# Where the sums of the first feed-forward's down projection read from, and the order of GpSimd's factor sums

## What is computed

```python
def swiglu(u, w_gate, w_up, w_down):
    return (jax.nn.silu(u @ w_gate) * (u @ w_up)) @ w_down
...
u = rmsnorm(h, ffn_norm[layer])
h = h + swiglu(u, *[p[layer] for p in ffn_p])
```

## Time and profile before

| | before |
|---|---|
| median of 3 runs | 3046.07 us (3045.73 to 3047.8) |
| profiled execution, its own time | 3044.75 us |
| its span, first to last instruction | 3042.9 us |
| PE busy | 2966.7 us (97%) |
| DVE, ACT, POOL busy | 1925.5, 1179.0, 1526.2 us |
| mean granted TensorE clock | 0.992 of full speed |

### The profile page before, as it was taken

How to read it: one execution, slowest core, us unless ns; L and a number is a source line. 1 busy time by engine, 2 the same in 40 slices (tenths; PEclk the granted TensorE clock), 3 DMA queues, 4 the chain that set the end, 5 groups by cost and what they waited for, 6 DMA issues and landing times. The chain is left out here.

```text
span 3042.9 us, 50019 instructions
## 1 busy us (share of the span) xinstructions
PE 2966.7 (97%) x19166; PEld 2684.6 (88%) x19166; DVE 1925.5 (63%) x2957; ACT 1179.0 (39%) x2029; POOL 1526.2 (50%) x996
## 2 busy tenths in 40 slices
PE   8999999999999999999999999899999999999997
PEld 8999999999999999999999978577777788887876
DVE  6677777754534446777788852677778844445665
ACT  4466666641333334553111122222323533334552
POOL 4100000043777777775444443567674577776673
PEclk9999999999999999999999999999999999999998
DMA  3000100021222324442233423332323132335442
GB/s 128 26 30 26 37 26 16 16 105 44 74 96 96 106 99 167 144 133 71 96 118 94 133 84 117 119 123 93 123 94 128 60 107 102 103 102 173 153 129 80
DMA packets 195934, 286.73 MB, mean 94 GB/s; under 512 B 14709, under 2 KB 105077, under 8 KB 195701
## 3 DMA queue, kind: packets, MB, share of 16 engines
q1 hardware_dynamic: 155952, 235.96, 23.4%
q10 hardware_dynamic: 39749, 47.60, 4.7%
HBM read 208.64 MB, written 74.86 MB: 93 GB/s over the span
## 5 line engine op out<-in xcount | busy, mean ns | idle before, releaser
L1248 PE MATMUL PS<-Uhi,Whi 128*128 128x352 f32 (+2 forms) x2024 | 511.5, 329 | 18.2 <-DVE Ulo L2771 13.7
L1248 PE MATMUL PS<-Uhi,Wlo 128*128 128x352 f32 (+2 forms) x2024 | 506.2, 326 | 0.0
L1248 PE MATMUL PS<-Ulo,Whi 128*128 128x352 f32 (+2 forms) x2024 | 506.0, 326 | 0.0
L1087 POOL TENSOR_TENSOR Wlo<-Wraw,Whi 128x512 fp32r<-128x512 f32 x241 | 328.3, 1365 | 140.5 <-ACT Whi L2414 136.9
L1248 PEld LDWEIGHTS PS<-Uhi,Whi 128*128 128x128 f32 x2024 | 340.2, 189 | 41.2 <-issue 18.2
L1046 POOL TENSOR_TENSOR Whi<-Wraw,const 128x1024 fp32r<-128x1024 f32 x64 | 159.6, 2494 | 417.5 <-PE PS L1248 402.7
L1248 PEld LDWEIGHTS PS<-Ulo,Whi 128*128 128x128 f32 x2024 | 343.3, 189 | 20.1
L1248 PEld LDWEIGHTS PS<-Uhi,Wlo 128*128 128x128 f32 x2024 | 342.8, 189 | 19.5
L2414 ACT ACTIVATE Whi<-Wraw 128x512 fp32r<-128x512 f32 x241 | 151.0, 629 | 339.5 <-POOL Wraw L1105 139.5
L1135 POOL TENSOR_TENSOR Olo<-H,Ohi 128x1056 fp32r<-128x1056 f32 x5 | 12.1, 2442 | 521.8 <-ACT Ohi L2317 521.8
L1248 PE MATMUL PS<-T,Whi 128*128 128x264 f32 (+1 forms) x1328 | 219.1, 288 | 2.0 <-DVE H L3283 1.9
(11 more groups left out here) (418 smaller groups left out, 7120.1 us busy)
## 6 DMA issues: line engine op xcount, KB each, us to landing
Wraw<-in_w SPq DMA_DIRECT2D x192, 256.0 KB, 2.9
Wraw<-in_w SPq DMA_DIRECT2D x91, 512.0 KB, 3.7
Wraw<-in_w SPq DMA_DIRECT2D x168, 128.0 KB, 2.6
xt<-XTT ACTq DMA_DIRECT2D x20, 640.0 KB, 5.7
opd<-HID SPq DMA_DIRECT2D x40, 264.0 KB, 3.4
T<-opd SPq DMA_DIRECT2D x18, 528.0 KB, 4.0
Ulo<-opd SPq DMA_DIRECT2D x17, 528.0 KB, 4.8
Ulo<-opd SPq DMA_DIRECT2D x17, 512.0 KB, 5.3
```

Of the source, the lines that this page charges most:

```text
L1087: pool.tensor_tensor(f.oplo[j % SLOTS], FIRST_S2 if (p, k) == (0, 6) else f.factors[k], f.ophi[j % SLOTS].bitcast(F32), ALU.subtract).then ...
L1248: ins = pe.matmul(out, lhsT, rhs, start=start, stop=stop, skip_group_check=True)
```

## The change

In the first feed-forward's last pair the product b12 is written to PSUM banks 0 and 1, which are empty there, instead of HID. `first_sum` and `second_sum` both read it from there, and both are done behind the second half's add, that of (5,0), the first one first. SP's stores of the two sums count the semaphore in the new order. The staging of operand 4, which uses the same banks, waits for the two sums. In both feed-forwards, GpSimd's order in the down rounds was low 1, S1, S2, S3, S4, low 5, low 6, low 3, low 7, low 2, low 4; it is now low 1, S1, S2, low 5, S3, S4, low 6, and on as before. In the pairs ahead of the down rounds the order stays.

```diff
--- before.py
+++ after.py
@@ -171,7 +171,7 @@
 UNSTAGED = 4
 WHOLE_LOWS, POOL_LOWS = (0, 1), (3, 2)
 LATE_LOWS = {4: 3, 5: 5, 6: 7}
-SECOND_AFTER, FIRST_AFTER, THIRD_AFTER, FOURTH_AFTER = 1, 2, 10, 11
+SUMS_AFTER, THIRD_AFTER, FOURTH_AFTER = 1, 10, 11
 WEIGHTS_HIGH = 10
 PLAIN_LOWS = (10, 12)
 
@@ -897,8 +897,7 @@
             if k in (1, 2, 3):
                 sp.wait_ge(f.quad_taken.sem, f.quad_taken.at(f.taken(p, {1: 0, 2: 2, 3: 3}[k])))
             else:
-                sp.wait_ge(f.sum_taken.sem, f.sum_taken.at(
-                    4 * i + ({7: 1, 5: 2, 6: 3, 4: 4} if f.first and p == LAST_PAIR else {5: 1, 7: 2, 6: 3, 4: 4})[k]))
+                sp.wait_ge(f.sum_taken.sem, f.sum_taken.at(4 * i + {5: 1, 7: 2, 6: 3, 4: 4}[k]))
             out = {1: f.quad_out[0], 5: f.quad_out[1], 4: f.quad_out[1], 7: f.quad_out[2], 3: f.quad_out[3],
                    6: f.quad_out[0] if f.first else f.t2_out, 2: f.b21_out}[k]
             sp.dma_start(f.opd[DOWN_ORDER.index(k), i // F_STEP][:, i % F_STEP * f.w:(i % F_STEP + 1) * f.w],
@@ -1101,6 +1100,10 @@
             pool.tensor_tensor(f.s1, r21, r22, ALU.add).then_inc(f.sum_made.sem, 1)
             pool.wait_ge(f.sum_made.sem, f.sum_made.at(4 * p + 1))
             pool.tensor_tensor(r21, r11, r21, ALU.subtract).then_inc(f.sum_made.sem, 1)
+
+        def third_sum(f, p):
+
+            r11 = f.raw[0]
             pool.wait_ge(f.sum_made.sem, f.sum_made.at(4 * p + 2))
             pool.tensor_tensor(r11 if p else FIRST_S2, f.s1, r11, ALU.subtract).then_inc(f.sum_made.sem, 1)
 
@@ -1114,18 +1117,22 @@
         def split_feed(f):
 
             factor_sums(f, 0)
+            third_sum(f, 0)
             fourth_sum(f, 0)
             for j, (p, k) in enumerate(f.products):
                 if k == 6 and 0 < p < PRODUCT_PAIRS:
                     factor_sums(f, p)
+                    third_sum(f, p)
                 if 0 < p < PRODUCT_PAIRS and k == ((2 if f.first else 5) if p == LAST_PAIR else 6):
                     fourth_sum(f, p)
                 low_factor(f, j)
+                if k == 5 and p >= PRODUCT_PAIRS:
+                    third_sum(f, p)
+                    fourth_sum(f, p)
                 if (p, k) in ((PRODUCT_PAIRS, 5), (PRODUCT_PAIRS, 3)) and f.pool_lows:
                     low_operand(f, f.pool_lows[k == 3])
                 if k == 1 and p >= PRODUCT_PAIRS:
                     factor_sums(f, p)
-                    fourth_sum(f, p)
             for n in range(F_STEP):
                 pool.wait_ge(f.prod_done.sem, f.prod_done.at(len(f.products) - 3 + 3 * n))
                 split((f.down + n) % 2)
@@ -2446,7 +2453,7 @@
             if f.first and g == 0 and o < UNSTAGED:
                 return
             if f.first and g == 0 and o == UNSTAGED:
-                act.wait_ge(f.quad_taken.sem, f.quad_taken.at(f.taken(LAST_PAIR - 1, 2)))
+                act.wait_ge(f.sum_taken.sem, f.sum_taken.at(4 * (LAST_PAIR // 2) + 2))
             elif g or o:
                 act.wait_ge(f.operand_ready.sem, f.operand_ready.at(f.ready_at(g, o) - 1))
             act.activation(PS[:, 0:F_STEP, :].rearrange("p b n -> p (b n)"),
@@ -3207,14 +3214,12 @@
 
             if not f.first:
                 return PS[:, 2:3, :]
-            return f.cut(f.hq[1]) if p == LAST_PAIR else f.bank(p, 3)
+            return PS[:, 0:2, 0:L // 2] if p == LAST_PAIR else f.bank(p, 3)
 
         def first_sum(f, p):
 
             x = b12_at(f, p)
             vec.wait_ge(f.quad_taken.sem, f.quad_taken.at(f.taken(p, 1)))
-            if f.first and p == LAST_PAIR:
-                vec.wait_ge(f.sum_taken.sem, f.sum_taken.at(4 * (p // 2) + 1))
             vec.tensor_tensor(f.cut(f.hq[1]), x, f.cut(f.hq[0]), ALU.subtract).then_inc(f.sum_taken.sem, 1)
 
         def second_sum(f, p):
@@ -3359,10 +3364,9 @@
             for sp in range(DOWN_PAIRS):
                 for k, x in HALVES:
                     take_half(f, sp, k, x)
-                    if n == SECOND_AFTER:
+                    if n == SUMS_AFTER:
+                        first_sum(f, p)
                         second_sum(f, p)
-                    if n == FIRST_AFTER:
-                        first_sum(f, p)
                     for low in lows.pop(n, ()):
                         low_part(f, *low)
                     if n == THIRD_AFTER:
```

## The result

| | before | after |
|---|---|---|
| median | 3047.0 us (6 runs, 3045.7 to 3049.0) | 3060.9 us (6 runs, 3058.5 to 3062.1) |
| ratio of the two | 1 | 1.0047, 95% interval 1.0037 to 1.0058 |
| profiled execution, its own time | 3044.75 us | 3059.91 us |
| its span | 3042.9 us | 3058.1 us |

The change makes the kernel 13.9 us slower. 6.0 were forecast, and the range ended at 3057. The direction and the chain were right; the amount was not.

The account below looks back on a forecast made before the run. The prediction took PE, busy 97% of the span, as the bound. It added 5.2 us (first feed-forward) and 0.8 (second) to 3044.75, giving 3050.8, or 3052.1 for the median; range about 3049.5 to 3057, with the faster rival from 3043.5.

Parts of the forecast that it names:

- The sums from PSUM: First feed-forward's last pair: b12's two sums take 0.68 and 0.69 us instead of 3.01 and 1.18, saving VectorE 2.8 us.
- the (5,1) gap: Round 0 of the first feed-forward: PE's 1.36 us gap at the weights of (5,1) goes.
- Rounds 0 and 1: First feed-forward: PE's 1.6 us earlier start of round 1 is taken back there; 0 us together, between -1.5 and +0.5.
- Even rounds: First feed-forward, rounds 2, 4, 6, 8: S3's 1.26 us delay reaches PE through the staging; 4.6 us lost.
- the spare time: Even rounds of the first feed-forward: the part of VectorE's staging wait that does not reach PE, taken as 0.78 us.
- Odd rounds: First feed-forward: staging behind high 3 is 1.26 us late; 0.3 us lost in rounds 3 and 5, none in 7: 0.6.
- The second feed-forward: Down rounds there: 1.3 us won, 1.4 lost to late staging, 0.7 to late quarter loads; sum +0.8.
- The cover: Rival: quarters land 0.8 to 1.3 us earlier against PE, hiding S3's delay; -3.6, 3042.5 us; 13%.
- the gains did not outweigh: Rival that gains and losses cancel: rounds 0 and 1 keep 1.6 us, odd rounds cost nothing; +1, 3047 us; 17%.
- the DMA case: Rival: low 7 late by 0.65 us makes every second feed-forward round that much longer; +9.9, 3056 us; 15%.
- the 1% rival: Rival: sums with b12 in PSUM take 3 us too, so rounds 0 and 1 are 1 us worse; 3053 us; 1%.

Follow-up runs that it names:

- e2: The kernel before with only the new place of S3 and S4 (behind low 5), b12's sums unchanged: ratio 1.0036 to before.
- e13: The changed kernel with the new order of the sums only in rounds 0 and 1 of the first feed-forward, the old one elsewhere: ratio 1.0003 to before.
- e4: The changed kernel with ScalarE rounding and staging the operand ahead of the high factor of its turn, from round 1 on: 3045.6 us, ratio 0.9997 to before.
- e1: The changed kernel with the old place of S3 and S4, so only b12's sums from PSUM remain: ratio 1.0005 to before.
- e7: The changed kernel with the new order of the sums in the second feed-forward alone, the old one in the first: ratio 1.0005 to before.
- s3: The kernel before, with GpSimd's low 5 of round 1 also waiting for VectorE's add of (1,0): a 2.36 us gap opened; no total time in the text.
- e3: The changed kernel with S3 and S4 of round 0 back in front of low 5, in both feed-forwards: ratio 1.0035 to before.
- e8: The changed kernel with the old order of the sums in rounds 0 and 1 of both feed-forwards, the new one from round 2: ratio 1.0029 to before.
- e10: e1 with staging ahead of the high factor from round 3 on: not faster than the kernel before; its ratio is not in the text.
- e5: e1 with ScalarE staging the operand ahead of the high factor of its turn, from round 1 on: ratio 0.9995 to before.

## Why the prediction was wrong

- **The sums from PSUM.** Right in the main: the first and the second sum took 0.70 and 0.69 us, the (5,1) gap went, the landing of the quarters took the gain back.
- **Rounds 0 and 1: 0, the term that failed.** It measured 3.8 us, in e2 4.3, in e13 3.8. The step reads: "In round 0 ScalarE makes high 5 about 1 us after S2's end; a GpSimd wait of up to 1 us there is half given back by less collision, and I count 0.1 at (6,0), inside the range above." The wait was named and sized rightly (1.12), and even more than half was given back (0.40 on low 5, S3 and S4, 0.46 on operand 3). But a second wait of 0.99, for the high part of operand 3 behind the late high 6, was missing, and I asked only who waits in the same round. GpSimd carried 1.2 us into low 3 and into the first quarter loads of round 1, whose landing I had let come "at best some 0.5 us earlier", never later. Then 1.1 us for the sums in round 1, which the forecast had as +0.1, and some 1.5 us of half clock, which it had not at all. 1.3 + 1.1 + 1.5 = 3.9.
- **Even rounds: 4.6.** The chain S3, high 6, staging, operand, (3,0) is right, and e4 shows it by cutting it. The waits were forecast at 2.5, 1.8, 2.3 and 1.9 us and measured 1.92, 1.80, 2.01 and 1.80; the gaps 1.8, 1.0, 1.5 and 1.1, measured 1.77, 1.62, 1.83 and 1.62, together 6.8 instead of 5.4; on the adds the four rounds lost 1.3, 1.7, 1.5 and 1.7, 6.2 instead of 4.6. Mis-sized is the spare time: 0.78 read off two rounds of before, 0.15 to 0.2 measured. The sum of the adds behind the staged operand, "0.61 + 0.61 + 0.72 + 0.55 + 0.80 + 0.70", took the small low part at the 0.55 of round 2, a value that hangs on where GpSimd stands; it became 1.2. This is read off the timing of the two engines in nine executions (0.62 to 0.64 in before, e1, e7, e13, s3; 1.23 to 1.28 in after, e2, e3, e8); no edit tried it.
- **Odd rounds: 0.6.** Round 3 has 1.16 us in two gaps, rounds 5 and 7 have none. Right in sum within 0.6, wrong in how it is spread. In e3 the small low part stayed at 0.19 in round 3, and there is no gap there.
- **The second feed-forward: 0.8.** 1.8 on the adds of these two executions, 2.6 with the clock put right, 2.1 by the comparison of eleven. The chain is the forecast one: the longest gap, 1.83 us in round 8 (forecast 1.4, the 0.3 of round 6 in it), stands at product 6, which waits for the add of (1,0), and this stood behind the staged operand. The view names GpSimd's low part, the one of product 3, since it ended 0.04 us later; product 6 doesn't read it. (VectorE's staged operand and four adds, PE's load, changed kernel:)

```profile
2974.71 1.23 DVE L3294 TENSOR_TENSOR T3r<-PS,T3r 128x1024 fp32r<-128x1024 f32 x1 [4.32 <-ACT PS L2459]
2975.85 2.47 DVE L3307 TENSOR_TENSOR H<-H,PS 128x512 f32<-128x512 f32 x4
```

```profile
2976.64 0.30 PEld L1255 LDWEIGHTS PS<-T1r,Whi 128*128 128x128 f32 x2 [1.83 <-POOL Wlo L1086]
```

Mis-sized were round 6 (1.04 for the forecast 0.3) and round 4 (0.57 for none), and round 7 kept gaps of 0.50 at product 5 and 0.65 at product 3 where none was forecast.

- **The rivals.** The cover was not found, the gains did not outweigh; the DMA case put its time down to quarter loads behind a late low 7, while the long gaps of rounds 4, 6 and 8 stand behind the staged operand; whether the loads lost time as well was not measured apart. Only the 1% rival had a loss in rounds 0 and 1, of 1 us, so the range ended 4 us short.

Forecast 6.0; the profiles show 3.8 + 7.0 + 2.6 = 13.4, and the medians 13.9. Single terms are known no better than to a microsecond, so part of this agreement is luck.

## What to carry to other kernels

When an instruction is moved within an in-order queue, follow everything behind it into the next round too, its DMA issues above all: here two waits of 1 us, less what came back, put 1.2 us on the first load of a burst, and its last landing was 1.3 us late. Look for the queue that ties two chains together without need; here the staging of an operand stood behind a factor that it doesn't use, and moving it by one place was worth 15 us to the changed kernel. A spare time read off one trace holds only while the other engines keep their places. And a gap at a place where PE is already waiting in pieces has to be priced with the clock in mind.

## What was not expected of the hardware

- 3.4 us (in e3 6.8) at a granted clock of 0.5 followed a gap of 2.66 us or more in round 1 in nine executions of nine; none followed gaps up to 2.36 there in the other nine, and none a gap of 2.73 alone in round 4. One came at a gap of 2.00 in round 0, in one execution (e2), and in round 0 of the second feed-forward a gap of 2.4 us had a stretch behind it in seven executions of fourteen. A stretch of 3.4 us in round 1 cost PE's matmuls 1.3 to 1.6 us (e10, e5, after, e13, e2).
- GpSimd's low 5 took 2.32 us in round 0 and 1.74 in round 1 of the changed kernel, where 1.29 is the time of an undisturbed low part. The Trainium skill (GPSIMD Engine Reference, Specifications) says that GpSimd shares its SBUF interfaces with VectorE; the spread of one and the same instruction by a factor of 1.8 agrees with it, and VectorE's low operands of the row at 1193.50, which ran beside low 5 of round 0, have two inputs from SBUF. By its place a moved instruction changes its length.
- The other way round it is sharper: a VectorE subtraction of 128x32 elements with two inputs from SBUF takes 0.19 us alone; started beside a GpSimd instruction of 1.3 us it ends 0.05 us behind that one, which makes up to 1.28 us in the changed kernel.
- The same code in unchanged stretches differs by up to 5 us from execution to execution through the places and numbers of the half-clock stretches (5.00 us at S1 of round 0), and eleven or more runs of one kernel on one chip spread over 8 to 15 us.
